# Third layer's steps: scores ahead of turns and values on TensorE, four buffers for weights instead of three

## The reference

```python
def even_mixer(h, w_in, ...):                      # third layer
    qa, ka, va, qi, ki, wi, qb, kvb, gb = split_cols(h @ w_in, EVEN_SPLITS)
    o_a = dsa_attention(rope(qa), rope(ka), va, ...)   # 8 heads, keys chosen by an index score
    o_b = nsa_attention(rope(qb), ...)                 # 8 heads: g0*compressed + g1*selected + g2*window
    return concatenate([o_a, o_b]) @ w_out

# each piece of attention, for 128 queries and n = 128..512 keys:
s = einsum('bqhd,bskd->bhqs', q, k) * scale        # scores
p = masked_softmax(s, mask)                        # weights: exp(s - max) / sum
o = einsum('bhqs,bshd->bqhd', p, v)                # values
```

## Time and profile before

| | before |
|---|---|
| median of 3 runs | 1815.64 us (1815.39 to 1815.89) |
| the profiled execution's own time | 1815.82 us |
| its span in the trace | 1814.0 us |
| TensorE busy | 1768.7 us (98%) |
| VectorE busy | 1153.6 us (64%) |
| ScalarE busy | 877.7 us (48%) |
| GpSimd busy | 477.5 us (26%) |

### The profile page before, as it was taken

How to read it: one execution, slowest core, us unless ns; L and a number is a source line. 1 busy time by engine, 2 the same in 40 slices (tenths; PEclk the granted TensorE clock), 3 DMA queues, 4 the chain that set the end, 5 groups by cost and what they waited for, 6 DMA issues and landing times.

```text
span 1814.0 us, 26417 instructions
## 1 busy us (share of the span) xinstructions
PE 1768.7 (98%) x10400; PEld 1460.7 (81%) x10404; DVE 1153.6 (64%) x1861; ACT 877.7 (48%) x1433; POOL 477.5 (26%) x467
## 2 busy tenths in 40 slices
PE   7999999999999999999999999999999999999997
PEld 6877777766887766777889898988888787989896
DVE  5355555577546688844577576765677657758574
ACT  5236665367535465564345252533445534535253
POOL 0035551015503055550220000005777114000000
PEclk9999999999999999999999999999999999999999
DMA  5321111232023321012232323222222123232322
GB/s 177 103 70 48 52 52 58 83 95 70 11 70 101 123 65 36 22 34 73 79 128 93 105 82 117 93 93 83 81 87 77 58 82 116 86 112 94 113 85 82
DMA packets 44522, 149.22 MB, mean 82 GB/s; under 512 B 6000, under 2 KB 6384, under 8 KB 44400
## 3 DMA queue, kind: packets, MB, share of 16 engines
q1 hardware_dynamic: 44400, 147.53, 24.7%
HBM read 139.64 MB, written 2.10 MB: 78 GB/s over the span
## 4 chain that ended last, share of the span: by engine, by line
PE 85%; DVE 6%; ACT 3%; POOL 2%; issue 2%; DMA 1%; POOLq 0%; SPq 0%; DVEq 0%; ACTq 0%
PE BANK L301 18%; PE BANK L303 18%; PE BANK L302 18%; PE BANK L2541 4%; PE BANK L2540 4%; PE BANK L2538 4%; PE BANK L688 2%; PE BANK L1875 1%; PE BANK L1856 1%; PE BANK L1832 1%; PE BANK L2871 1%; PE BANK L1054 1%; PE BANK L673 1%; PE BANK L2846 1%; DVE WL L278 1%
## 5 line engine op out<-in xcount | busy, mean ns | idle before, releaser
L269 ACT ACTIVATE WH<-WRAW 128x1024 fp32r<-128x1024 f32 (+1 forms) x214 | 223.1, 1044 | 325.1 <-PE BANK L303 293.6
L278 DVE TENSOR_TENSOR WL<-WRAW,WH 128x1024 fp32r<-128x1024 f32 (+1 forms) x201 | 256.9, 1279 | 135.1 <-ACT WH L269 134.8
L301 PE MATMUL BANK<-HH,WH 128*128 128x512 f32 x664 | 273.7, 412 | 10.4 <-DVE WL L278 9.6
L303 PE MATMUL BANK<-HL,WH 128*128 128x512 f32 x664 | 260.3, 392 | 0.0
L302 PE MATMUL BANK<-HH,WL 128*128 128x512 f32 x664 | 260.0, 392 | 0.0
L301 PE MATMUL BANK<-HIDH,WH 128*128 128x512 f32 (+1 forms) x520 | 201.2, 387 | 1.7 <-issue 1.5
L302 PE MATMUL BANK<-HIDH,WL 128*128 128x512 f32 (+1 forms) x520 | 200.7, 386 | 0.0
L303 PE MATMUL BANK<-HIDL,WH 128*128 128x512 f32 (+1 forms) x520 | 200.7, 386 | 0.0
L2541 PE MATMUL BANK<-HP,G 128*128 128x256 f32 x672 | 190.2, 283 | 0.0
L2540 PE MATMUL BANK<-HP,G 128*128 128x256 f32 x672 | 190.2, 283 | 0.0
L2538 PE MATMUL BANK<-HP,G 128*128 128x256 f32 x672 | 190.1, 283 | 0.0
(11 more groups left out here) (497 smaller groups left out, 3762.0 us busy)
## 6 DMA issues: line engine op xcount, KB each, us to landing
WRAW<-in_w SPq DMA_DIRECT2D x77, 512.0 KB, 3.5
WRAW<-in_wd SPq DMA_DIRECT2D x64, 512.0 KB, 3.5
RAW<-in_wf SPq DMA_DIRECT2D x32, 512.0 KB, 3.5
WRAW<-in_wu SPq DMA_DIRECT2D x16, 512.0 KB, 3.5
TMP<-in_wf SPq DMA_DIRECT2D x16, 512.0 KB, 3.5
WRAW<-in_w0o SPq DMA_DIRECT2D x8, 512.0 KB, 3.6
WRAW<-in_w1o SPq DMA_DIRECT2D x8, 512.0 KB, 3.6
WRAW<-in_wc SPq DMA_DIRECT2D x8, 512.0 KB, 3.4
```

The costliest lines, as they stand in the source:

```text
L269: e.activation(WH[b % NS][:, 0:n], WRAW[b % NR][:, 0:n], ACT.Copy).then_inc(*inc("s_high", ("high", b)))
L278: e.tensor_tensor(WL[b % NS][:, 0:n], WRAW[b % NR][:, 0:n], WH[b % NS][:, 0:n].bitcast(F32), ALU.subtract).then_inc(*inc("s_low_pool" if p ...
L301: e.matmul(dst, ah, bh, start=first and i == 0, stop=False)
L303: made = e.matmul(dst, ah, bl, start=False, stop=last and i == len(sets) - 1)
```

## The change

TensorE's loop now begins a step with `scores(s)`; `turn(s-4)` and `values(s-5)` follow it, then the filler as before. A fourth buffer for exponentials, `EPD`, is laid into free room of the shared region, and units take the buffers by u mod 4; the wait for the old unit's turn follows that number. The other engines' loops stay as they were. All lines behind the new one at 187 carry numbers one higher.

```diff
+        EPD = alias([("under_epd", [128, 46 * T], F32), ("EPD", [128, 2 * T], F32)])[1]
...
-            return SCR[:, 1024 * (u % 3):1024 * (u % 3) + 1024].rearrange("p (b n) -> p b n", b=2)
+            return (EPD if u % 4 == 3 else SCR[:, 1024 * (u % 4):1024 * (u % 4) + 1024]).rearrange("p (b n) -> p b n", b=2)
...
             for step in range(E_N + E_VALUES):
+                if step < E_N:
+                    scores(step)
                 if 0 <= step - E_TURN < E_N:
                     turn(step - E_TURN)
                 if step >= E_VALUES:
                     values(step - E_VALUES)
-                if step < E_N:
-                    scores(step)
...
-                before = [x for x in range(u) if x % 3 == u % 3 and e_units[x][0] != "c"]
+                before = [x for x in range(u) if x % 4 == u % 4 and e_units[x][0] != "c"]
```

## The result

| | before | after |
|---|---|---|
| median | 1815.77 us (1815.39 to 1816.3, 4 runs) | 1841.74 us (1840.85 to 1842.43, 4 runs) |
| ratio to before | | 1.0143, 95% interval 1.0131 to 1.0156 |
| profiled execution, span | 1815.82, 1814.0 us | 1841.38, 1839.6 us |

The change costs 26 us; 20.4 had been forecast, with a range from 1826 to 1845. It lies wholly in the third layer's steps. From the first score matmul to the last value matmul before took 829.2 - 649.3 = 179.9 us, and after takes 854.7 - 648.7 = 206.0, 26.1 more. The groups of L1832 and L1875, and of L1833 and L1876, give these starts: before

What follows compares the result with a forecast made beforehand. TensorE, busy 98% of the span, was taken to bound the kernel; 28 us lost in score waits less 8 gained gave +20 on 1815.6, 1835.6, and 1836 us with short half-clock stretches; range 1826 to 1845.

Steps and rivals of the forecast that it cites:

- The fourth buffer: nothing: ScalarE's exponentials: the copy queued ahead already waits for the same turn, so the fourth buffer costs and gains 0.
- The chain D against the cover C: From turn(s-4)'s end to scores(s+1): ScalarE's copy and exponentials (D) outlast TensorE's values and filler (C); 28.0 us lost.
- the list: Score waits forecast step by step for steps 4 to 50, 43 places, numbered by the step before; sum 28.0 us.
- VectorE falls late: Rival: VectorE late at six projections and behind compressed units' reciprocals, up to 1 us ten times, +5 to +8; 10%.
- The copy and the turn as its cause: ScalarE's copy of turn(s-4) stands ahead of the exponentials that scores(s+1) needs, and waits for that turn.
- The gain of 8 us: In front of turns and values: 5.3 us of waits, 1.0 of restarts and 1.5 of half clock go; 7.8, rounded.
- No other cost: TensorE's steps: no instruction added, removed or reshaped; the new order itself was given no price.
- Half clock: TensorE at 1.2 GHz: the old stretch's 1.5 us goes; one or two short new stretches lift 1835.6 to 1836 us.
- the sum: TensorE's third-layer steps: 28 us lost in score waits less 8 gained at turns and values, +20 us on 1815.6.
- one or two short stretches: TensorE's new half-clock stretches not hidden by the waits; they take the forecast from 1835.6 to 1836 us.
- The rival of half clock: Half clock returns more often, behind five waits of 1.3 us or more: up to +7.5, 1844 to 1845 us; 15%.

Runs made afterwards that it cites:

- the buffer alone: The change with TensorE's old order (turn, values, scores), so only the fourth exponentials buffer added to the kernel before: 1815.23 us, ratio 0.9998.
- the order alone: The kernel before with only TensorE's loop changed to scores, turn, values, keeping three exponentials buffers: 1840.64 us, ratio 1.0134.
- the maxima alone: The whole change, with VectorE's maxima of unit s moved from step s+1 into step s, ScalarE's order unchanged: 1839.29 us, ratio 1.0128.
- exponentials first, maxima early: The whole change, with ScalarE's exponentials ahead of the copy of turned weights and VectorE's maxima of unit s in step s: 1819.61 us, ratio 1.002.
- the scores between turn and values: The whole change, but with TensorE's order turn, scores, values: 1828.24 us, ratio 1.0068.
- the exponentials first: The whole change, with ScalarE's exponentials put ahead of the copy of turned weights in each step: 1832.47 us, ratio 1.0091.

## Why the prediction was right, point by point

- *The fourth buffer: nothing.* Right, shown by the buffer alone (0.9998) and by the order alone, 1840.64 us.
- *The chain D against the cover C.* Right. The chain and its links are there, at step 11 with 1.97 us for 2.00. The three longest waits stand at the places that the list gives. 24.3 us in 31 places are recorded, where near 25 in some 34 were forecast; the list's 28.0 counts from start to start, which takes in the restart behind each wait. At step 30 the wait is 2.39 for 1.63, because the exponentials waited 0.75 us for the maxima. The rival "VectorE falls late" shows in three more places, the scores of steps 15, 22 and 33, which waited 0.48, 0.19 and 0.37 us more than the list has; against them, the 0.95 us listed for the scores of step 46 did not appear. So the total fits better than single places do.
- *The copy and the turn as its cause.* Shown in the end, but not by one kernel: with the copy out of the way the waits fell by 10 us, with the maxima early too by 22.7 of 24.3, and with the maxima alone by 2.2.
- *The gain of 8 us.* Right in kind: no wait in front of turns or values is left. Its size can't be read apart from the loss.
- *No other cost.* Wrong: the prediction has "No instruction is added or removed, and none takes another shape" and gave the order itself no price. With 0.7 us fewer recorded waits than before and no half clock, the steps in the new order take 4.0 us more, and some 1.5 more if before's one stretch of half clock is taken off: about 5.5 to 6 us. The trace places 3.6 of them, behind the filler; the rest was not located.
- *Half clock.* Under-sized: the sum takes off 1.5 us for the stretch of before and puts in 0.4 for "one or two short stretches", 1.1 us less in all. There are two stretches more than before, up to 1.7 us each, so up to 3.4 us more: the term is up to 4.5 us out. The rival of half clock, priced at up to +7.5 beyond the forecast, is in part what happened.

The two terms together, 5.5 to 6 us for the order and up to 4.5 for the clock, are more than the 5.7 us between 20.4 forecast and 26.1 measured. What stands against them is in the waits: in the steps they come to 25.0 us, before to 7.1, 17.9 more, where the sum had 28.0 - 6.3 = 21.7. The comparison is rough, since the recorded waits leave out the restart behind each. So the mechanism was foreseen, but it is in part luck that the time came out inside the range: two costs were missing or too small, and the waits cost less than the sum had.

## What to carry to other kernels

Before moving a stage forward on one engine, list what its first instruction waits for and follow that wait back through the other engines' queues: here the scores' banks hang on exponentials, these on a copy queued ahead of them, and that on a turn that the move had put directly in front. The cover between the two ends is what counts, and it can be summed step by step from one trace; here the sum came to 28.0 us, against 24.3 recorded in 31 waits with a restart behind each, while single places were out by up to 0.95 us. A buffer adds nothing as long as a queue's order imposes the same wait, and queue orders on several engines have to be moved together. Even then compare what follows what on the full engine: with all the queues moved, the new order was still 0.2% slower than before.

## What the runs showed of the hardware

A score matmul (64 rows of weights) starts 0.327 us behind a 512-column matmul of 128 rows (exponentials first, maxima early), where a transpose (128 rows) starts 0.231 behind it (before), both without a recorded wait. In the profile of the change the three stretches at 1.2 GHz in these steps stood right behind single waits of TensorE of 1.69, 2.39 and 2.02 us, in work that is otherwise dense, while its next longest wait, 1.42 us at step 5, had none behind it. In the kernel before the one stretch stands behind a wait of 1.51 us; the same wait had none behind it with the buffer alone (1.51 us) and with the scores between turn and values (1.50 us). With the exponentials first a stretch began at 673.6 us, where the waits before it were 0.38 us (to 671.04) and 0.16 us (to 668.24). So the length of a wait does not by itself tell whether a stretch follows.
